# Layer 0 of a four-layer transformer: the stick-breaking heads move ahead of the causal heads, and the rotary turn moves in beside them

## The chip, the cores and the metric

The kernel runs on one core of one Trainium2 chip. The time is the device time of the whole program in microseconds (us). Five engines work from queues of their own: PE (TensorE, matrix products), DVE (VectorE), ACT (ScalarE), POOL (GpSimd) and SP (SyncE, which here only issues the loads of weights). They meet only at semaphores. TensorE runs at one of two clocks, 1.2 or 2.4 GHz; the profile gives the granted clock of a stretch as a share of 2.4 GHz, so 0.50 means 1.2 GHz.

## What is computed

Two blocks of two layers each over 512 tokens of width 1024. The change touches only the mixer of layer 0. It has 8 causal softmax heads with a rotary turn of queries and keys, and 8 stick-breaking heads without one (the causal heads' block selection is, at 512 tokens and two blocks, plain causal attention). The turn is x1\*cos - x2\*sin and x2\*cos + x1\*sin on the first 16 of a head's 64 dimensions:

```python
def attention_head_groups(h, positions, w_in, w_out):
    proj = h @ w_in
    qa, ka, va, qb, kb, vb = (t.reshape(B, T, -1, HEAD_DIM) for t in jnp.split(proj, cuts, axis=-1))
    qa = partial_rope(qa, positions)
    ka = partial_rope(ka, positions)
    oa = moba_attention(bhtd(qa), bhtd(ka), bhtd(va))
    ob = stick_breaking_attention(bhtd(qb), bhtd(kb), bhtd(vb))
    ...
    return o @ w_out

# stick-breaking, per block of 128 queries
z = einsum(q, k) * dh ** -0.5
log_1m = where(causal, log_sigmoid(-z), 0.0)
log_after = cumsum(log_1m, reverse=True) - log_1m
w = where(causal, exp(log_sigmoid(z) + log_after), 0.0)
out = einsum(w, v)
```

## The kernel before, in words

Everything lies transposed: channels on the 128 partitions, the 512 tokens along the row. The program of each engine is written out by hand, stage by stage. At the end of a stage `ph.end` drains the engine, counts up one semaphore and waits until PE, ACT, DVE and POOL have all done so: a barrier of four engines. SP has no part in it; it loads weight tiles into a ring of four slots as they come free.

Layer 0 runs these stages, each closed by such a barrier:

1. **Projection** (`pe_attn_in`, `act_attn_in`, `dve_attn_in`, lines 887 to 932). 12 weight tiles. ACT rounds tile m+1 (`next_own`, line 364), POOL takes the rest of it (line 376), PE multiplies in three passes (tiles 0 to 7 give QK1, 16 chunks of 128 channels; tiles 8 to 11 give V1, lines 420 to 422), and ACT copies the result out of PSUM (lines 918, 925). DVE weighs the adaptive-norm tiles. Before that, `dve_angles` has made the angles of the rotary turn in COS1 and SIN1 and has signalled `angles_ready`.
2. **Rotary stage** (lines 2174, 2243 to 2247, 2313 to 2314). ACT scales the stick heads' queries (QK1 chunks 8 to 11) by 0.125, takes the sine of both tables in place and puts a sign on SIN1 (`angles_done`). For each of the 8 chunks of causal queries and keys PE multiplies by a permutation (`pe_rope`, two fp32 passes of 512 columns, four PSUM buffers), and DVE does three operations of 512 columns: swapped times sin, chunk times cos, sum (`dve_rope`, lines 1194 to 1196).
3. **Causal heads** (`pe_attention`, `dve_attention`, `act_attention` over `causal_jobs`). 32 jobs, a head and 128 queries each. PE: scores (line 1034), transposes of the weights (1043), outputs (1054). DVE: scale and mask (1090, 1092), maximum (1099), reciprocal (1116), weights (1126). ACT: exponential (1152), copy of the transposes (1160), copy of the head (1167). DVE computes scores three jobs ahead before it makes the first job's weights.
4. **Stick heads** (`pe_stick`, `act_stick`, `dve_stick`, `pool_stick`, lines 1250 to 1349). Per head h, PE runs `z` (scores, line 1258, 8 instructions), `sums` (running sums by a triangle of ones, line 1268, 20 instructions) and `outputs` (line 1279, 8 instructions), in the order z(h+1), sums(h), outputs(h-1). z has two PSUM buffers; z(h) waits until ACT's `weights` of head h-2 has read its buffer (`sticks_read`). ACT runs `softplus(h+1)` (Abs, Exp, Ln over 1280 columns, lines 1299 to 1301), then `weights(h)` (Exp, line 1308), then the copy of head h-1 (line 1313). DVE has one operation a head (line 1330), POOL masks (line 1338). WORK is shared by the stages, so the barrier is needed between them.
5. **Output projection** (`pe_out`, `act_out` with a preloading of the set `natural_log_exp_and_others`, line 485, and so on).

The queues of ACT and the table sets: an activation whose function isn't in the loaded set of tables is preceded by a table load (ACT_TABLE_LOAD in the profile), placed when the program is built. `preload_act_table_set` loads a named set.

Of the kernel before, what the change touches and what calls it, by code (L numbers as in the profile page):

```python
# [9 lines left out]
ALU = mybir.AluOpType  # L10
# [81 lines left out]
def build_program(nc, w_tiles, d_tiles, xT, ctxT, positions, consts, params, rope_tables, outT):  # L92
# [12 lines left out]
    with ctx:  # L105
# [77 lines left out]
        def sig(name):  # L183

            if name not in scratch:
                scratch[name] = sem(name)
            return scratch[name]
# [721 lines left out]
                mm.then_inc(tile_done, 1)  # L909
                pe_ada_tile(pe, 0, m + ADA // 2, m % 2)  # L910

        def act_attn_in(act):
            g0 = G0["attn_in"]

            def features(m, v, i):
                next_own(act, "attn_in", round_tile, m, 2 * v, i)
                act.wait_ge(tile_done, i * 4 + (g0 + 2 * v + 1))
                act.activation(QK1[:, bass.ds(m * 2, 2), :],
                               PS[:, v * 1024:(v + 1) * 1024].rearrange("p (j c) -> p j c", j=2),
                               ACT.Copy).then_inc(evac_done, 1)  # L920
            over_pairs(act, 8, features, lambda m, v, i: None)
            for m in range(8, 12):
                next_own(act, "attn_in", round_tile, m, 2 * m, 0)
                act.wait_ge(tile_done, g0 + 2 * m + 1)
                act.activation(V1[:, :, (m - 8) * 256:(m - 7) * 256],
                               PS[:, (m % 2) * 1024:(m % 2 + 1) * 1024].rearrange("p (a c) -> p a c", a=NT),
                               ACT.Copy).then_inc(evac_done, 1)
# [322 lines left out]
        def pe_stick(pe):  # L1250
            def z(h):
                if h >= 2:
                    pe.wait_ge(sig("sticks_read"), h - 1)
                r = slice((h % 2) * 64, (h % 2) * 64 + 64)
                for i in (0, 1, 3, 2):
                    a, w = sb_bank(h, i), T - i * P

                    mm = pe.matmul(PS[:, a:a + w], QK1[r, 12 + h // 2, i * P:(i + 1) * P],
                                   QK1[r, 8 + h // 2, i * P:T], start=i != 3, stop=True, skip_group_check=True)
                mm.then_inc(sig("z_ready"), 1)  # L1260

            def sums(h):
                pe.wait_ge(sig("softplus_masked"), h + 1)
                for i in (0, 1, 3, 2):
                    for j in range(i, NT):
                        a = sb_bank(h, i) + (j - i) * P
                        w = T - j * P
                        mm = pe.matmul(PS[:, a:a + w], const("negtri") if j == i else const("negones"),
                                       SP_[h % 2][:, OFFS[j]:OFFS[j] + w], start=False, stop=True, skip_group_check=True)
                mm.then_inc(sig("sticks_ready"), 1)  # L1270

            def outputs(h):
                pe.wait_ge(sig("sticks_masked"), h + 1)
                if h >= 2:
                    pe.wait_ge(sig("stick_heads_copied"), h - 1)
                off = (h % 2) * 64
                for i in range(NT):
                    o = 3072 + (h % 2) * 512
                    mm = pe.matmul(PS[off:off + 64, o + i * P:o + T], V1[:, i, 512 + h * 64:512 + (h + 1) * 64],
                                   SW[h % 2][:, OFFS[i]:OFFS[i] + T - i * P], start=i == 0, stop=i == NT - 1,  # L1280
                                   skip_group_check=True)
                mm.then_inc(sig("stick_heads_ready"), 1)

            z(0)
            for h in range(8):
                if h + 1 < 8:
                    z(h + 1)
                sums(h)
                if h >= 1:
                    outputs(h - 1)  # L1290
            outputs(7)

        def act_stick(act, chain):
            def softplus(h):
                act.wait_ge(sig("z_ready"), h + 1)
                if h >= 2:
                    act.wait_ge(sig("sticks_ready"), h - 1)
                L, a = SP_[h % 2], (h % 2) * 1536
                chain(act.activation(L, PS[:, a:a + SBW], ACT.Abs))
                chain(act.activation(L, L, ACT.Exp, scale=-1.0))  # L1300
                act.activation(L, L, ACT.Ln, bias=SM[:, 1:2]).then_inc(sig("log_ready"), 1)

            def weights(h):
                act.wait_ge(sig("sticks_ready"), h + 1)
                if h >= 2:
                    act.wait_ge(sig("stick_heads_ready"), h - 1)
                a = (h % 2) * 1536
                act.activation(SW[h % 2], PS[:, a:a + SBW], ACT.Exp).then_inc(sig("sticks_read"), 1)

            def copy(h):  # L1310
                off = (h % 2) * 64
                act.wait_ge(sig("stick_heads_ready"), h + 1)
                act.activation(H[off:off + 64, 4 + h // 2, 0:T], PS[off:off + 64, 3072 + (h % 2) * 512:3072 + (h % 2) * 512 + T],
                               ACT.Copy).then_inc(sig("stick_heads_copied"), 1)

            softplus(0)
            for h in range(8):
                if h + 1 < 8:
                    softplus(h + 1)
                weights(h)  # L1320
                if h >= 1:
                    copy(h - 1)
            copy(7)

        def dve_stick(dve):
            for h in range(8):
                dve.wait_ge(sig("log_ready"), h + 1)
                a = (h % 2) * 1536

                dve.scalar_tensor_tensor(out=SP_[h % 2], in0=PS[:, a:a + SBW], scalar=0.0, in1=SP_[h % 2],  # L1330
                                         op0=ALU.max, op1=ALU.add).then_inc(sig("softplus_ready"), 1)

        def pool_stick(pool):
            def keep_past(buf):
# [15 lines left out]
        def rope1_chunks():  # L1350
            return [(QK1[:, x, :], const("perm_a1"), COS1, SIN1) for x in range(8)]
# [812 lines left out]
        def _(pe):  # L2164
            ph = Phase()
            pe.wait_ge(consts_loaded, 16)
            for layer in range(4):
                segs = SEG1 if layer < 2 or layer == LAST else SEG2
                if layer == 0:
# [1 line left out]
                    pe_norm_sum(pe, 0, T)  # L2171
                    pe_attn_in(pe)
                    ph.end(pe)
                    pe_rope(pe, rope1_chunks())
                    ph.end(pe)
                    pe_attention(pe, causal_jobs())
                    ph.end(pe)
                    pe_stick(pe)
                    ph.end(pe)
                    pe_out(pe, "attn_out", SEG1)  # L2180
                elif layer == 1:
# [35 lines left out]
        def _(act):  # L2217
# [5 lines left out]
            for layer in range(4):  # L2223
# [14 lines left out]
                    for k in range(DC):  # L2238
                        act_norm_chunk(act, [CTX] if layer == LAST else [MAIN, CTX], mod[:, 0:DC, :], k, "chunk_shifted")
                if layer == 0:  # L2240
                    act_attn_in(act)
                    ph.end(act)
                    act.wait_ge(sig("angles_ready"), 1)
                    act.activation(QK1[:, 8:12, :], QK1[:, 8:12, :], ACT.Copy, scale=0.125)
                    chain(act.activation(COS1, COS1, ACT.Sin))
                    chain(act.activation(SIN1, SIN1, ACT.Sin))
                    act.activation(SIN1, SIN1, ACT.Copy, scale=const("sign")).then_inc(sig("angles_done"), 1)
                    ph.end(act)
                    act_attention(act, causal_jobs(), chain)
                    ph.end(act)  # L2250
                    act_stick(act, chain)
                    ph.end(act)
                elif layer == 1:
                    act_gdn_in(act)
# [36 lines left out]
        def _(dve):  # L2291
# [6 lines left out]
            for layer in range(4):  # L2298
# [10 lines left out]
                if layer == 0:  # L2309
# [1 line left out]
                    dve_attn_in(dve, chain)  # L2311
                    ph.end(dve)
                    dve.wait_ge(sig("angles_done"), 1)
                    dve_rope(dve, rope1_chunks(), chain)
                    ph.end(dve)
                    dve_attention(dve, causal_jobs(), chain)
                    ph.end(dve)
                    dve_stick(dve)
                    ph.end(dve)
                    dve_out(dve, "attn_out", mod[:, 2 * DC:3 * DC, :], SEG1)  # L2320
                elif layer == 1:
# [38 lines left out]
        def _(pool):  # L2360
            ph = Phase()
            for layer in range(4):
                segs = SEG1 if layer < 2 or layer == LAST else SEG2
                if layer == 0:
                    for k in range(DC - 1):
                        pool_add(pool, k, T)
                    rest_tile(pool, "attn_in", 0, 0, 0)
                    pool_rest(pool, "attn_in")
                    ph.end(pool)
                    ph.end(pool)  # L2370
                    ph.end(pool)
                    pool_stick(pool)
                    ph.end(pool)
                elif layer == 1:
                    rest_halves(pool, 0, 0)
                    pool_gdn_in(pool)
                    ph.end(pool)
                    pool_gdn_prep(pool)
                    ph.end(pool)
                    for grp in range(2):  # L2380
                        pool_gdn_inverse(pool, grp)
                        ph.end(pool)
                        ph.end(pool)
                    ph.end(pool)
                else:
                    for _ in range(6):
                        ph.end(pool)
# [186 lines left out]
```

## Time and profile before

| | |
|---|---|
| median of 3 timed runs | 4042.73 us (4042.47 to 4046.4) |
| profiled execution: its time | 4048.2 us |
| profiled execution: span of the core | 4046.3 us |
| mean granted clock over the span | 0.927 |
| PE busy | 3630.5 us (90%) |
| DVE, ACT, POOL busy | 1887.5, 1249.2, 1060.4 us (47%, 31%, 26%) |
| layer 0's mixer: projection ends, rotary, causal, stick, output projection begins | 238.4, 258.0, 369.5, 462.8 us |

Busy times and durations are those of one profiled execution. A PE that is busy isn't a PE at its peak: at 1.2 GHz the same matmul keeps it busy nearly twice as long. In the rows below, "x8" counts instructions that the timeline has merged; the bracket at a row's end is how long the engine had been idle before it and what ended that.

### The profile page before, as it was taken

The numbers are of one execution on the slowest core, as the hardware profiler recorded it, in microseconds if no ns is written. First come the engines' busy times: TensorE is split into PE (matmuls) and PEld (weight loads), VectorE is DVE, ScalarE is ACT, GpSimd is POOL, SyncE is SP. The second block draws the span as 40 slices with busy tenths as digits, with TensorE's granted clock in tenths as the row PEclk, the third lists the DMA queues.
The fourth block names the chain that finished last, engine by engine and source line by source line (L and its number), as shares of the span: only waits on it lengthen the run. The fifth ranks groups of instructions, "written<-read, shape, count | busy, mean of one in ns | idle before, by whom it ended". The sixth has DMA issues, their size and how long they took to land. (4 is left out here: it accounts for less than half of the span.)

```text
span 4046.3 us, 46564 instructions
## 1 busy us (share of the span) xinstructions
PE 3630.5 (90%) x17568; PEld 2825.1 (70%) x17568; DVE 1887.5 (47%) x3523; ACT 1249.2 (31%) x1790; POOL 1060.4 (26%) x611
## 2 busy tenths in 40 slices
PE   2989999999967879999998978899999998879998
PEld 2865678878656758886575546788899566557887
DVE  7343242437354457473607683654345517662111
ACT  2224532223321132123004544222244104443222
POOL 2300334444424333433000002334400000014444
PEclk9975999999988989999997978999999997779999
DMA  6410134432200014342110001334445210002221
GB/s 229 166 73 1 42 139 147 187 120 89 88 1 1 1 52 175 142 169 96 52 66 8 1 1 42 114 144 173 148 164 172 73 73 1 1 32 83 89 98 64
DMA packets 54942, 355.62 MB, mean 88 GB/s; under 512 B 5888, under 2 KB 6912, under 8 KB 19456
## 3 DMA queue, kind: packets, MB, share of 16 engines
q1 hardware_dynamic: 54496, 351.35, 23.7%
q8 instruction: 107, 1.75, 0.2%
q10 hardware_dynamic: 288, 2.10, 0.1%
q14 instruction: 51, 0.42, 0.0%
HBM read 351.32 MB, written 2.10 MB: 87 GB/s over the span
## 5 line engine op out<-in xcount | busy, mean ns | idle before, releaser
L376 POOL TENSOR_TENSOR W_LO<-ring,W_HI 128x2048 fp32r<-128x2048 f32 (+1 forms) x177 | 730.3, 4126 | 1095.2 <-ACT W_HI L364 1095.2
L432 PE MATMUL PS<-H_HI,W_HI 128*128 128x512 f32 (+1 forms) x1888 | 713.4, 378 | 32.6 <-DVE H_LO L810 26.3
L434 PE MATMUL PS<-H_HI,W_LO 128*128 128x512 f32 (+1 forms) x1888 | 703.4, 373 | 0.0
L433 PE MATMUL PS<-H_LO,W_HI 128*128 128x512 f32 (+1 forms) x1888 | 703.3, 373 | 0.0
L364 ACT ACTIVATE W_HI<-ring 128x2048 fp32r<-128x2048 f32 (+1 forms) x214 | 366.2, 1711 | 444.6 <-PE PS L422 444.3
L432 PEld LDWEIGHTS PS<-H_HI,W_HI 128*128 128x128 f32 x1888 | 359.7, 191 | 98.6 <-issue 37.6
L434 PEld LDWEIGHTS PS<-H_HI,W_LO 128*128 128x128 f32 x1888 | 359.3, 190 | 63.4
L433 PEld LDWEIGHTS PS<-H_LO,W_HI 128*128 128x128 f32 x1888 | 360.0, 191 | 59.5 <-issue 0.2
L852 DVE SCALAR_TENSOR_TENSOR PS<-ring,SC,PS 128x256 f32<-128x256 f32 x792 | 388.0, 490 | 27.8
L420 PE MATMUL PS<-HID_HI,W_HI 128*128 128x512 f32 (+1 forms) x880 | 325.3, 370 | 4.9 <-DVE W_LO L376 4.0
L422 PE MATMUL PS<-HID_HI,W_LO 128*128 128x512 f32 (+1 forms) x880 | 323.7, 368 | 0.0
L421 PE MATMUL PS<-HID_LO,W_HI 128*128 128x512 f32 (+1 forms) x880 | 323.7, 368 | 0.0
L521 POOL TENSOR_TENSOR W_LO<-ring,W_HI 128x512 fp32r<-128x512 f32 x16 | 23.2, 1452 | 1121.6 <-ACT W_HI L511 1121.3
L592 ACT ACTIVATE GATED<-PS 128x512 f32<-128x512 f32 (+1 forms) x110 | 61.1, 555 | 724.4 <-PE PS L434 724.4
L283 PE MATMUL PS<-H,ring 128*128 128x512 f32 (+1 forms) x800 | 278.2, 511 | 6.0 <-ACT H L960 6.0
L607 DVE TENSOR_TENSOR HIDDEN<-GATED,PS 128x512 f32<-128x512 f32 (+1 forms) x110 | 69.8, 634 | 424.2 <-ACT GATED L592 424.2
L1034 PE MATMUL PS<-BIG 64*128 64x256 f32 (+5 forms) x640 | 245.8, 625 | 10.6 <-DVEq L243 7.6
L283 PEld LDWEIGHTS PS<-H,ring 128*128 128x128 f32 x800 | 152.8, 191 | 131.8 <-issue 122.2
L729 DVE SCALAR_TENSOR_TENSOR X<-PS,MOD,X 128x512 f32<-128x512 f32 (+1 forms) x80 | 55.7, 696 | 387.8 <-PE PS L422 387.8
L1054 PEld LDWEIGHTS PS<-WORK,BIG 128*64 128x64 f32 x1312 | 172.8, 162 | 90.7 <-issue 53.3
L1054 PE MATMUL PS<-WORK,BIG 128*64 128x128 f32 x1312 | 218.3, 322 | 18.6 <-ACT WORK L1160 18.3
L1160 ACT ACTIVATE WORK<-PS 128x768 f32<-128x768 f32 (+5 forms) x152 | 96.0, 631 | 314.6 <-PE PS L1043 314.5
(280 smaller groups left out, 5674.1 us busy)
## 6 DMA issues: line engine op xcount, KB each, us to landing
ring<-w_tiles SPq DMA_DIRECT2D x273, 1024.0 KB, 4.8
ring<-d_tiles SPq DMA_DIRECT2D x80, 704.0 KB, 4.1
X<-xT SPq DMA_DIRECT2D x1, 2048.0 KB, 19.3
WORK<-rope_tables ACTq DMA_DIRECT2D x2, 1024.0 KB, 6.9
outT<-H SPq DMA_DIRECT2D x8, 256.0 KB, 2.2
CN<-consts SPq DMA_DIRECT2D x1, 1377.0 KB, 15.8
X<-ctxT SPq DMA_DIRECT2D x1, 1024.0 KB, 21.5
PR<-params SPq DMA_DIRECT2D x1, 465.5 KB, 3.4
```

Of the source, the lines that this page charges most:

```text
L283: mm = pe.matmul(PS[:, o:o + w], ring[:, slot, k * 256 + j * P:k * 256 + (j + 1) * P], src[:, k, c0:c0 + w], start=k == 0, stop=k == DC - 1)
L364: act.activation(W_HI[:, b, 0:w], ring[:, g % SLOTS, 0:w], ACT.Copy).then_inc(sig("tile_rounded"), 1)
L376: eng.tensor_tensor(W_LO[:, b, 0:w], ring[:, g % SLOTS, 0:w], W_HI[:, b, 0:w].bitcast(F32), ALU.subtract).then_inc(sig("tile_split"), 1)
L420: pe.matmul(PS[:, o:o + w], hi(k), x_hi(k), start=k == 0, stop=False)
L421: pe.matmul(PS[:, o:o + w], hi(k), x_lo(k), start=False, stop=False)
L422: mm = pe.matmul(PS[:, o:o + w], lo(k), x_hi(k), start=False, stop=k == n - 1)
L432: pe.matmul(to, hi[:, cols(k, j)], x_hi(k), start=k == 0, stop=False)
L433: pe.matmul(to, hi[:, cols(k, j)], x_lo(k), start=False, stop=False)
L434: mm = pe.matmul(to, lo[:, cols(k, j)], x_hi(k), start=False, stop=k == n - 1)
L852: ins = dve.scalar_tensor_tensor(out=out, in0=w, scalar=c[:, k:k + 1], in1=acc, op0=ALU.mult, op1=ALU.add)
L1034: mm = pe.matmul(PS[:, a:a + k.shape[-1]], job["q"][m], k, start=True, stop=True)
L1054: mm = pe.matmul(PS[off:off + 64, o:o + P], v, PT[n % 2][:, x * P:(x + 1) * P], start=x == 0, stop=x == len(job["v"]) - 1)
```

## The change

The stick heads become the second stage, and the rotary stage is gone as a stage of its own:

- The scaling of the stick queries moves into ACT's projection loop, after the rounding at m == 9. The two sines and the sign move there too, after the rounding at m == 10, in a new function `act_sines`, which ends with a preload of the set `natural_log_exp_and_others`.
- `pe_stick` gets `swap(n)`: the permutation product of causal chunk n = h, issued between z(h+1) and sums(h), into PSUM columns 3584 to 4095. From n = 1 it waits for `swap_read`, DVE's reading of the chunk before.
- To make room for it, the stick heads' outputs use one PSUM bank at 3072 rather than two; even and odd heads still lie on different halves of the partitions.
- `dve_stick` gets `rotate(n)`, the three operations of the turn for chunk n = h, right after the head's one operation.
- The order of stages on all engines is projection, stick, causal, output projection: three barriers instead of four.

```diff
+        def act_sines(act, chain):
+            act.wait_ge(sig("angles_ready"), 1)
+            chain(act.activation(COS1, COS1, ACT.Sin))
+            chain(act.activation(SIN1, SIN1, ACT.Sin))
+            act.activation(SIN1, SIN1, ACT.Copy, scale=const("sign")).then_inc(sig("angles_done"), 1)
+            act.preload_act_table_set("natural_log_exp_and_others")
...
             for m in range(8, 12):
                 next_own(act, "attn_in", round_tile, m, 2 * m, 0)
+                if m == 9:
+
+                    act.wait_ge(evac_done, E0["attn_in"] + 8)
+                    act.activation(QK1[:, 8:12, :], QK1[:, 8:12, :], ACT.Copy, scale=0.125)
+                if m == 10:
+                    act_sines(act, chain)
...
-                    o = 3072 + (h % 2) * 512
+                    o = 3072
...
+            def swap(n):
+
+                if n:
+                    pe.wait_ge(sig("swap_read"), n)
+                chunk, perm, _, _ = rope1_chunks()[n]
+                pe.matmul(PS[:, 3584:3584 + T], perm, chunk, start=True, stop=True).then_inc(sig("head_swapped"), 1)
+
             z(0)
             for h in range(8):
                 if h + 1 < 8:
                     z(h + 1)
+                swap(h)
                 sums(h)
...
-        def dve_stick(dve):
+        def dve_stick(dve, chain):
+            def rotate(n):
+                c, _, cos, sin = rope1_chunks()[n]
+                tmp = ROPE_TMP[:, (n % 2) * T:(n % 2) * T + T]
+                dve.wait_ge(sig("head_swapped"), n + 1)
+                dve.tensor_tensor(tmp, PS[:, 3584:3584 + T], sin, ALU.mult).then_inc(sig("swap_read"), 1)
+                chain(dve.tensor_tensor(c, c, cos, ALU.mult))
+                dve.tensor_tensor(c, c, tmp, ALU.add)
+
...
+                rotate(h)
...
-                    pe_rope(pe, rope1_chunks())
+                    pe_stick(pe)
                     ph.end(pe)
                     pe_attention(pe, causal_jobs())
-                    ph.end(pe)
-                    pe_stick(pe)
                     ph.end(pe)
```

The programs of ACT, DVE and POOL are put in the same order.

## Rows read from the trace of the kernel before

**Rows 1.** The page, part 1: busy time of TensorE over the span.
```profile
PE 3630.5 (90%) x17568; PEld 2825.1 (70%) x17568; DVE 1887.5 (47%) x3523; ACT 1249.2 (31%) x1790; POOL 1060.4 (26%) x611
```

**Rows 2.** Windows by stage: length, busy PE, PEld, DVE, ACT, POOL, clock, DMA, GB/s.
```profile
200.00:238.00 38.00, 37.62 (x316) 37.53 (x314) 8.12 (x18) 7.36 (x6) 9.24 (x2) 1.00 0.43 166
238.00:258.00 20.00, 10.76 (x16) 3.24 (x16) 15.47 (x26) 4.12 (x5) 0.00 (x0) 0.78 0.14 52
258.00:369.00 111.00, 106.07 (x304) 59.22 (x304) 49.79 (x152) 40.81 (x128) 0.00 (x0) 0.50 0.00 1
369.00:462.00 93.00, 81.95 (x289) 47.76 (x288) 11.93 (x8) 65.56 (x56) 16.60 (x64) 0.87 0.00 0
```

**Rows 3.** Timeline of the rotary stage: start, length, engine, line, operation.
```profile
238.43 3.70 PE L1186 MATMUL PS<-BIG,CN 128*128 128x512 f32 x8 [0.81 <-ACTq L243]
238.51 1.91 ACT L2244 ACTIVATE BIG<-BIG 128x2048 f32<-128x2048 f32 x1 [0.17 <-POOLq L243]
...
241.64 0.72 ACT L2247 ACTIVATE BIG<-BIG,CN 128x512 f32<-128x512 f32 x1
242.45 0.69 DVE L1194 TENSOR_TENSOR WORK<-PS,BIG 128x512 f32<-128x512 f32 x1 [4.17 <-ACTq L243]
243.06 0.68 DVE L1195 TENSOR_TENSOR BIG<-BIG 128x512 f32<-128x512 f32 x1
243.77 0.69 DVE L1196 TENSOR_TENSOR BIG<-BIG,WORK 128x512 f32<-128x512 f32 x1
...
257.26 0.69 DVE L1196 TENSOR_TENSOR BIG<-BIG,WORK 128x512 f32<-128x512 f32 x1
258.05 4.64 PE L1034 MATMUL PS<-BIG 64*128 64x128 f32 x10 [5.67 <-DVEq L243]
```

**Rows 4.** Timeline of ACT in the projection, m == 10: the rounding and the copy.
```profile
214.32 1.91 ACT L364 ACTIVATE W_HI<-ring 128x2048 fp32r<-128x2048 f32 x1
225.36 1.03 ACT L925 ACTIVATE BIG<-PS 128x1024 f32<-128x1024 f32 x1 [9.13 <-PE PS L422]
```

**Rows 5.** Groups by line, stick stage: ACT's table loads, busy and mean ns.
```profile
L1301 ACT ACT_TABLE_LOAD x8 | 10.3, 1283 | 0.1
...
L1308 ACT ACT_TABLE_LOAD x7 | 9.0, 1283 | 0.1
```

**Rows 6.** Timeline of the stick stage: one head's round on PE and ACT.
```profile
424.16 4.60 PE L1268 MATMUL PS<-WORK,CN 128*128 128x512 f32 x20
424.27 1.24 ACT L1299 ACTIVATE WORK<-PS 128x1280 f32<-128x1280 f32 x1 [1.76 <-PE PS L1258]
...
428.69 2.37 PE L1279 MATMUL PS<-WORK,BIG 128*64 128x512 f32 x8
...
430.80 1.24 ACT L1308 ACTIVATE WORK<-PS 128x1280 f32<-128x1280 f32 x1
...
432.08 2.42 PE L1258 MATMUL PS<-BIG 64*128 64x512 f32 x8 [1.02 <-ACT WORK L1308]
...
434.55 1.24 ACT L1299 ACTIVATE WORK<-PS 128x1280 f32<-128x1280 f32 x1 [1.90 <-PE PS L1258]
```

**Rows 7.** Timeline of the stick stage: its first head on ACT and PE.
```profile
374.23 1.24 ACT L1299 ACTIVATE WORK<-PS 128x1280 f32<-128x1280 f32 x1 [4.82 <-PE PS L1258]
...
382.28 3.93 PE L1268 MATMUL PS<-WORK,CN 128*128 128x512 f32 x7 [5.00 <-POOL WORK L1338]
```

**Rows 8.** Windows: where the clock falls and where it comes back.
```profile
246.00:250.00 4.00, 3.56 (x4) 1.01 (x4) 3.93 (x7) 0.00 (x0) 0.00 (x0) 0.50 0.00 0
...
384.00:389.00 5.00, 4.50 (x19) 3.13 (x17) 1.49 (x1) 3.55 (x4) 1.04 (x4) 0.84 0.00 0
```

**Rows 9.** Timeline of the causal stage: its first transpose on PE.
```profile
264.77 0.47 PE L1043 MATMUL PS<-CN,WORK 128*128 128x128 f32 x1 [2.09 <-DVE WORK L1126]
```

**Rows 10.** Windows of layer 2's attention, early and late in its stage.
```profile
2160.00:2180.00 20.00, 16.95 (x75) 11.95 (x74) 13.07 (x39) 5.81 (x15) 0.00 (x0) 0.50 0.00 0
...
2240.00:2260.00 20.00, 18.93 (x109) 12.57 (x108) 14.07 (x30) 10.49 (x26) 0.00 (x0) 1.00 0.01 2
```

More of the change, by code:

```diff
@@ L910, in pe_attn_in, with act_attn_in @@
                 pe_ada_tile(pe, 0, m + ADA // 2, m % 2)
-        def act_attn_in(act):
+        def act_sines(act, chain):
[4 more added lines that the diff above has]
+            act.preload_act_table_set("natural_log_exp_and_others")
+        def act_attn_in(act, chain):
             g0 = G0["attn_in"]
@@ L1312, in copy @@
                 act.wait_ge(sig("stick_heads_ready"), h + 1)
-                act.activation(H[off:off + 64, 4 + h // 2, 0:T], PS[off:off + 64, 3072 + (h % 2) * 512:3072 + (h % 2) * 512 + T],
+                act.activation(H[off:off + 64, 4 + h // 2, 0:T], PS[off:off + 64, 3072:3072 + T],
                                ACT.Copy).then_inc(sig("stick_heads_copied"), 1)
@@ L2240, in _ @@
                 if layer == 0:
-                    act_attn_in(act)
+                    act_attn_in(act, chain)
                     ph.end(act)
[L2243 to L2247, printed above, removed]
+                    act_stick(act, chain)
                     ph.end(act)
                     act_attention(act, causal_jobs(), chain)
-                    ph.end(act)
-                    act_stick(act, chain)
                     ph.end(act)
@@ L2313, in _ @@
                     dve.wait_ge(sig("angles_done"), 1)
-                    dve_rope(dve, rope1_chunks(), chain)
+                    dve_stick(dve, chain)
                     ph.end(dve)
                     dve_attention(dve, causal_jobs(), chain)
-                    ph.end(dve)
-                    dve_stick(dve)
                     ph.end(dve)
@@ L2369, in _ @@
                     ph.end(pool)
+                    pool_stick(pool)
                     ph.end(pool)
-                    ph.end(pool)
-                    pool_stick(pool)
                     ph.end(pool)
```

## The prediction, made before the changed kernel was run

> **What bounds the kernel now.** I read the views in this order: the page, the windows by stage, then the timelines of the stages that move. Over the whole span TensorE is busy nine tenths [rows 1], but the change moves only stages in which it isn't the one limit. The windows by stage are read one against the other [rows 2]: the projection's end keeps TensorE full at 2.4 GHz; the rotary stage lasts 20 us with TensorE busy 10.8; the causal stage lasts 111 us with TensorE busy 106 but at 1.2 GHz throughout; the stick stage lasts 93 us with TensorE busy 82 and ACT 66.
>
> The rotary stage is bound by DVE: TensorE starts at 238.43, DVE starts its first product at 242.45 and its last sum at 257.26, and the causal scores start at 258.05 [rows 3]. The first 4 us are ACT's scaling and sines, 238.51 to 242.36; the rest is 8 chunks of three DVE operations.
>
> In the stick stage a head's round is read on PE and ACT side by side [rows 6]. From sums to sums PE runs sums 4.5 (424.16 to 428.69), outputs 2.4, then idles 1.02 for ACT's weights, then z 2.4. On ACT the round from Abs to Abs is 434.55 - 424.27 = 10.28 us; from Abs to the weights it is 430.80 - 424.27 = 6.53, and two table loads of 1.283 are in it [rows 5]. So ACT's chain with its loads sets the pace by 1.02 us over PE's own work of 9.26.
>
> **The rotary stage as a stage: -19.6.** It goes with its barrier: 258.05 - 238.43 = 19.62 us [rows 3]. What it did must now hide elsewhere.
>
> **Scaling and sines in the projection: 0.** The four operations took 242.36 - 238.51 = 3.85 us [rows 3]: 1.91 of scaling, 1.94 of sines and sign. The new load adds 1.28 [rows 5]. At m == 10 ACT rounds at 214.32 and then idles 9.13 before the copy at 225.36 [rows 4]; the sines and the load need 3.2 of that, at m == 9 the scaling 1.9 of the like gap. They stand behind the rounding on ACT's queue, so POOL and the next tile don't wait for them; behind them stands only the copy. If that cover were gone it would cost 5.1 us. `angles_ready` came before the projection, so that wait is free.
>
> **Swap on PE: +1.0 a head, into a gap of 1.02.** The 8 merged rotary instructions took 3.70 us, about 0.43 apart at full clock [rows 3]; a swap is two of them and a change of weights, 0.9 to 1.1; I take 1.0. The next z behind it waits for the weights anyway.
>
> **Table loads in the stick stage: off ACT, and PE takes over as the limit.** The 15 loads of these two lines, and one more for the first Exp of head 1, are 16 x 1.283 = 20.5 us of ACT [rows 5]. After the preload Exp and Ln are in one set. From Abs to weights ACT then needs 6.53 - 2.57 = 3.96 us. PE needs, from the end of z, swap 1.0 and sums 4.5 = 5.5, so weights start when the sums end. While ACT takes 1.24 for them, PE runs outputs for 2.4, and the 1.02 us of idle [rows 6] is gone. The new round is PE's own: 2.4 + 1.0 + 4.5 + 2.4 = 10.25 us against 10.28. Of 20.5 us taken off ACT, nothing comes out in the steady rounds; it pays for the swap. Even if the loads stayed, the swap would fit the old gap.
>
> **DVE in the stick stage: 0.** A rotate is three operations a little over 0.6 apart, 1.9 to 2.0 us [rows 3]. It waits for `head_swapped`, 1.0 after the end of z, and so ends 3.0 after it; the next softplus comes off ACT at 3.96. Queued behind the wait is only that operation. DVE is busy 12 of the 93 us there [rows 2] and would become 28.
>
> **Start of the stick stage: -3.7, of which I take -3.0.** ACT's first Abs came at 374.23 after 4.82 us of waiting, since z ran at 1.2 GHz; z takes 2.4 at full clock [rows 6, 7], and the stage now follows the projection at 2.4 GHz: -2.4. One table load of the first softplus is on the way to the first sums (8.05 us after the first Abs, 382.28 - 374.23 [rows 7]): -1.28. Against it: PE then has z of head 1 and a swap, 3.4 us, to fill 6.8, and idles 3.4. In the rotary stage TensorE was done at 242.13, could go on only after DVE's first sum at 244.46, and was at 1.2 GHz from 246 on [rows 3, 8], and in the stick stage of before it came back at the first sums [rows 8]. A fall in the first two heads costs up to 4.7 us (sums at half clock), before had some of this too. Bounds: -4.7 and +1.
>
> **Causal stage: -0.5.** It did not show a start at full clock, so I bound this. It begins with scores and then waits until DVE has scores for three jobs: the first transpose came at 264.77, 6.7 us after the stage began, mostly DVE's work [rows 3, 9]. Scores at full clock may take 1.5 us off, or nothing. After these sparse microseconds I expect 1.2 GHz as before, for the remaining 104 us. The stage's table load for Exp falls away too, beside DVE's lead. The output projection starts from 1.2 rather than 2.4 GHz, but waits for its weight pieces first: 0, plus or minus 1.5.
>
> **Sum.** -19.6 + 0 + 0 - 3.0 - 0.5 = -23.1 us. The profiled execution's 4048.2 becomes 4025.1. It lies 5.5 above the median of the three runs, so for the median: 4042.7 - 23.1 = 4019.6. A measurement of this kernel can tell about 0.2%, 8.1 us, from no change. The forecast's own range adds the bounds (-27.8 to -17.1) and 2 us for the spread of the runs, 3.9 us from first to last: 4013 to 4028.
>
> What a table load costs is where the skill and the trace part. The trace leaves it 1.283 us: in 6.53 us there are two loads and three activations of at least 1.24 each, 6.3 in all, with 0.2 left [rows 5, 6]. The Trainium skill (ScalarE: Activation LUTs, What ACT_TABLE_LOAD costs) adds a drain of about 1.38 us to each switch of sets, 2.66 in all. By it the first softplus would gain 2.66 rather than 1.28 and the sum would be -24.5; the rows leave no room for it.
>
> **Rivals.**
>
> *The causal stage gets the full clock.* Price: a head takes TensorE 106.07 / 8 = 13.3 us at 1.2 GHz [rows 2]. At 2.4 GHz that halves to 6.6, DVE has 49.79 / 8 = 6.2, and the hand-overs between them stay; I estimate 8. Each warm head saves 5.3 us, 7 of them 37: 3982; if the clock rises half way, about 18: 4001. For it: in layer 2 the same attention program stood at 1.2 GHz early in its stage and at 2.4 GHz later, with PE busy 17 of 20 us before and 19 after [rows 10], and PE is as busy in the causal stage. Now that stage is entered at full clock rather than from the idle of the rotary stage. Against: it stayed at 0.50 for all of its 111 us [rows 2], the clock fell in the rotary stage after a shorter sparse stretch than the one before the first transpose [rows 3, 8, 9], and its jobs are smaller than layer 2's. By the Trainium skill (TensorE: Matmul & The Clock Gate, Part 4: PE-mode transpose) transposes don't count as busy in the way that other matmuls do, which would make this case rarer. Layer 2 holds the full clock with transposes in every job [rows 10], so I leave the chance as it is. 20%.
>
> *The turn isn't hidden.* If DVE's three operations came between one head's softplus and the next (a wait for the swap that comes late, with the head's masking behind it), each head would pay about 2 us: 16 in all, 4035.6. Against: the order above leaves 1 us of slack, DVE is nearly idle. 5%.
>
> *Slower: the stick stage loses the clock for good.* Its rounds are now PE's own work. If the idle of the first head brings TensorE to 1.2 GHz and it stays there, a round is nearly twice 10.25; z went from 2.4 to 4.8 us between the clocks [rows 6, 7]. That is about 9 us a head, 72 in all: 4092. It takes more than two and a half heads at half clock (23.1 / 9) before the change loses. Against: before entered this stage at 1.2 GHz and got 2.4 within the first sums [rows 8]. 3%.
>
> That the change doesn't do what it says, the loads staying, gives about 1.3 us less and is in the forecast's range.
>
> **How the numbers follow.** Forecast 72% (4013 to 4028), warm causal stage 20% (3980 to 4012), turn not hidden 5%, slower 3%. The range 3988 to 4028 holds most of the first and over half of the second. Faster by over 0.2% is the first two, 92%; within 0.2% the third, 5%; slower 3%.
>
> **What would show it.** Right: no line between the projection's end and z; first Abs about 2.5 us into the stick stage; rounds of 10.2 to 10.3 us with no table load and no idle of PE before z; stick stage 89 to 92 us; causal stage 110 us at 0.50. Wrong: clock above 0.5 in the causal stage, which alone can move the time by more than 10 us; PE waiting for DVE's reading of the swap; DVE's rotate ending after the next Ln; or the projection's tiles more than 12 us apart.

## The result, and the profile after

| | before | after |
|---|---|---|
| time, median (lowest to highest) | 4044.57 us (4042.47 to 4048.43, 4 runs) | 3994.16 us (3986.77 to 4020.85, 4 runs) |
| profiled execution, its time | 4048.2 us | 3992.96 us |
| causal stage, its length | 110.6 us | 77.5 us |
| stick stage, its length | 92.4 us | 89.8 us |
| rotary stage | 19.6 us | gone |

The ratio is 0.9886, with a 95% interval of 0.984 to 0.9933. In the profiled executions the stages account for the difference: 19.6 of the rotary stage, 2.6 of the stick stage, 33.1 of the causal stage, together 55.3 us; the times differ by 4048.2 - 3992.96 = 55.2. (What lies outside these stages differs by 1 to 2 us in either direction and cancels here.) So the largest part came from a stage whose work, but for one table load, was not touched. Two executions of later variants that took 6913.64 and 13174.75 us, far above the rest of their kernel's, are left out of the medians below. A stage is measured from its first matmul to the start of its last one.

The page of the changed kernel, part 1, which answers to [rows 1]. ACT has 16 instructions and 20.8 us less, the table loads that went:

```profile
PE 3586.6 (90%) x17568; PEld 2805.6 (70%) x17568; DVE 1888.4 (47%) x3523; ACT 1228.4 (31%) x1774; POOL 1060.9 (27%) x611
```

Windows by stage of the changed kernel, with the columns of [rows 2]: the projection's end, the stick stage, then the causal stage in four parts:

```profile
200.00:236.00 36.00, 36.00 (x302) 35.94 (x301) 7.82 (x16) 11.75 (x11) 9.26 (x2) 1.00 0.45 176
236.00:327.00 91.00, 83.51 (x305) 48.25 (x304) 28.28 (x35) 45.65 (x41) 17.60 (x64) 0.94 0.03 12
327.00:332.00 5.00, 3.36 (x10) 1.40 (x10) 3.53 (x11) 2.36 (x7) 0.00 (x0) 1.00 0.00 0
332.00:360.00 28.00, 26.97 (x77) 14.92 (x77) 14.28 (x45) 9.61 (x31) 0.00 (x0) 0.51 0.00 1
360.00:380.00 20.00, 19.46 (x95) 10.75 (x96) 15.48 (x49) 13.34 (x44) 0.00 (x0) 1.00 0.01 2
380.00:406.00 26.00, 22.07 (x124) 13.56 (x124) 15.73 (x49) 15.22 (x49) 0.00 (x0) 1.00 0.00 1
```

The third column from the end is the clock. Before, it was 0.50 for all 111 us of the causal stage. Here it falls 5 us after the stage begins, as the forecast had it, but it is back at full from 360 on, which the forecast did not have. In the half-clock window 77 matmuls take 26.97 us, in the next 95 take 19.46.

ACT in the projection, m == 10 and the tile after, which answers to [rows 4]:

```profile
214.52 0.62 ACT L914 ACTIVATE BIG<-BIG 128x512 f32<-128x512 f32 x1
...
216.58 1.28 ACT L917 ACT_TABLE_LOAD   x1
223.76 1.02 ACT L938 ACTIVATE BIG<-PS 128x1024 f32<-128x1024 f32 x1 [5.89 <-PE PS L422]
```

The sines and the load stand in the wait ahead of the copy, and 5.89 us of that wait are left. The copies of three tiles start at 211.80, 223.76 and 235.72: 11.96 apart, and so were they before (213.40, 225.36, 237.32).

The start of the stick stage, all engines, which answers to [rows 3] and [rows 7]:

```profile
236.83 4.04 PE L1271 MATMUL PS<-BIG 64*128 64x512 f32 x16 [0.81 <-ACTq L243]
239.35 1.24 ACT L1320 ACTIVATE WORK<-PS 128x1280 f32<-128x1280 f32 x1 [2.61 <-PE PS L1271]
...
245.04 1.96 POOL L1368 TENSOR_SCALAR_AFFINE_SELECT WORK<-WORK 128x128 f32<-128x128 f32 x4 [25.72 <-DVE WORK L1359]
245.41 0.72 DVE L1352 TENSOR_TENSOR BIG<-BIG 128x512 f32<-128x512 f32 x1
...
247.06 3.35 PE L1281 MATMUL PS<-WORK,CN 128*128 128x512 f32 x4 [5.14 <-POOL WORK L1368]
```

z follows the projection's barrier, the first Abs comes 2.5 us in, and the first sums wait for POOL's four masks, which run while DVE turns the first chunk of causal queries.

One round in its middle, which answers to [rows 6]:

```profile
279.82 4.50 PE L1281 MATMUL PS<-WORK,CN 128*128 128x512 f32 x20
...
284.24 2.37 PE L1292 MATMUL PS<-WORK,BIG 128*64 128x512 f32 x8
284.35 1.24 ACT L1329 ACTIVATE WORK<-PS 128x1280 f32<-128x1280 f32 x1 [1.46 <-PE PS L1281]
286.54 2.42 PE L1271 MATMUL PS<-BIG 64*128 64x512 f32 x8
288.89 1.12 PE L1302 MATMUL PS<-BIG,CN 128*128 128x512 f32 x2
289.00 1.24 ACT L1320 ACTIVATE WORK<-PS 128x1280 f32<-128x1280 f32 x1 [1.76 <-PE PS L1271]
```

No bracket stands behind a line of PE, so PE waits for nobody, and ACT now waits for PE twice a round (1.46 and 1.76). DVE's part, in the same round:

```profile
281.34 0.69 DVE L1353 TENSOR_TENSOR BIG<-BIG,WORK 128x512 f32<-128x512 f32 x1
282.93 1.49 DVE L1359 SCALAR_TENSOR_TENSOR WORK<-PS,WORK 128x1280 f32<-128x1280 f32 x1 [0.89 <-ACT WORK L1322]
```

The last step of the turn ends at 282.03 and DVE then waits 0.89 for the next softplus, about the 1 us of slack that was forecast. The round, Abs to Abs, is 289.00 - 278.96 = 10.04 us.

### The profile page after: what moved, and what is told of

Read it like the earlier page. It is cut to its first block and busy times, and to the rows that moved or that the text cites. A ratio compares the mean times of both kernels' runs of the same rounds, so it can differ in the third digit from the quotient of the medians.

```text
span 3990.8 us, 46542 instructions
## 1 busy us (share of the span) xinstructions
PE 3586.6 (90%) x17568; PEld 2805.6 (70%) x17568; DVE 1888.4 (47%) x3523; ACT 1228.4 (31%) x1774; POOL 1060.9 (27%) x611
## 5 line engine op out<-in xcount | busy, mean ns | idle before, releaser
L852 DVE SCALAR_TENSOR_TENSOR PS<-ring,SC,PS 128x256 f32<-128x256 f32 x792 | 388.0, 490 | 27.8
L1047 PE MATMUL PS<-BIG 64*128 64x256 f32 (+5 forms) x640 | 229.9, 593 | 5.6 <-DVE WORK L1103 2.2
L1067 PE MATMUL PS<-WORK,BIG 128*64 128x128 f32 x1312 | 202.6, 306 | 19.8 <-ACT WORK L1173 19.6
L1067 PEld LDWEIGHTS PS<-WORK,BIG 128*64 128x64 f32 x1312 | 161.3, 153 | 82.4 <-ACT WORK L1173 45.8
L420 PEld LDWEIGHTS PS<-HID_HI,W_HI 128*128 128x128 f32 x880 | 165.9, 188 | 34.6 <-DVE W_LO L376 5.3
```

Of the source, the lines that this page charges most:

```text
L420: pe.matmul(PS[:, o:o + w], hi(k), x_hi(k), start=k == 0, stop=False)
L852: ins = dve.scalar_tensor_tensor(out=out, in0=w, scalar=c[:, k:k + 1], in1=acc, op0=ALU.mult, op1=ALU.add)
L1047: mm = pe.matmul(PS[:, a:a + k.shape[-1]], job["q"][m], k, start=True, stop=True)
L1067: mm = pe.matmul(PS[off:off + 64, o:o + P], v, PT[n % 2][:, x * P:(x + 1) * P], start=x == 0, stop=x == len(job["v"]) - 1)
```

## Experiments

**The same kernel again, and the spread of the runs.** The expectation:

> The changed kernel once more, unaltered, for the spread of its times. Theory A (the causal stage of layer 0 gets the full clock at a point that differs from run to run; in the first profile it rose after two of its eight heads): times lie in two groups or a band, near 4021 us where the stage stays at 1.2 GHz and from 3985 to 4005 us where it rises, and the mean granted clock of a run goes with its time (0.926 in the slow ones, 0.936 to 0.940 in the others). Rival B (the stage rises because it is entered from the stick stage, always at the same place): all runs within 4 us of each other, near 3990 us.

Measured: a median of 4019.02 us over 6 runs, 3991.63 to 4024.77; ratio 0.991 (0.9884 to 0.9936). The profiled one was 4024.1 us. Its windows, the first microseconds of the causal stage and the rest:

```profile
326.00:330.00 4.00, 3.40 (x10) 1.40 (x10) 2.80 (x9) 1.55 (x6) 0.00 (x0) 0.95 0.02 4
330.00:436.00 106.00, 101.39 (x294) 56.62 (x294) 46.72 (x144) 38.43 (x123) 0.00 (x0) 0.50 0.00 0
```

This is the forecast's case: the stage lasted 109.3 us, the stick stage 88.2. A third set of the same kernel:

> The changed kernel unaltered, for more of its times. So far 5 of 10 runs near 3987 to 3998 and 5 near 4018 to 4025; of the kernel before, 9 of 40 runs below 4041. If the share of runs with the rise is the same for both kernels (a quarter): 1 to 4 of some ten runs below 4010. If entering the stage at full clock helps: half of them or more.

Measured: 3993.83 us, 6 runs of 3990.97 to 3997.77, none of the other sort; ratio 0.9882 (0.9844 to 0.9921). In its profile the clock is low at the same place and comes back at 372, after the third head:

```profile
331.00:372.00 41.00, 40.13 (x114) 22.18 (x114) 20.32 (x64) 14.40 (x47) 0.00 (x0) 0.50 0.00 0
372.00:410.00 38.00, 34.26 (x181) 20.12 (x180) 25.12 (x78) 23.53 (x75) 0.00 (x0) 1.00 0.00 1
```

All 16 runs of the changed kernel fall in two groups: 11 between 3986.8 and 3997.8 (median 3993.6), 5 between 4018.0 and 4024.8 (median 4020.85), nothing between. The three profiles put the groups down to the causal stage: 77.5 us (3992.96), 83.1 us (3994.06) and 109.3 us (4024.1). The share differs from set to set: 3 of 4, 2 of 6, 6 of 6. The second and the third were taken on different chips, so that a part of the difference may be the chip's or the hour's.

The kernel before was run beside every experiment: of 71 runs, 54 lie above 4041 (median 4046.8), 7 between 3999.0 and 4011.1, 10 between 4027.5 and 4040.0. No trace of one of the 17 faster ones was kept. That the clock rose in them, in the 10 later than in the 7, is inferred: their mean granted clocks are 0.934 to 0.942 in the 7 and 0.928 to 0.931 in the 10, and 0.922 to 0.929 in all but one of the 50 slower ones for which it is on record. Beside the third set of the changed kernel, where 6 of 6 rose, 2 of 14 of the kernel before lay below 4041; beside the second, where 2 of 6 rose, it was 4 of 19.

**The order alone.** Causal and stick stage change places on PE, ACT, DVE and POOL (here PE); the rotary stage, the loads and the sines stay:

```diff
+                    pe_stick(pe)
+                    ph.end(pe)
                     pe_attention(pe, causal_jobs())
-                    ph.end(pe)
-                    pe_stick(pe)
```

> The kernel before with the causal and the stick stage exchanged and nothing else: the rotary stage stands where it did, the table loads stay. The causal stage is now entered at 2.4 GHz from the stick stage. Theory A (where the clock rises is a matter of where the stage falls in time, not of what stood ahead of it): most runs within 5 us of before, some up to 35 us faster. Rival B (entering from the stick stage is what warms it): 20 to 35 us faster in nearly every run. Rival C (the order itself gives the start of the stick stage at full clock): 2 to 3 us at the most, causal stage at 0.50.

Measured: 4047.1 us, 11 runs; ratio 0.9995 (0.9983 to 1.0008). Two of the 11 were at 4020.9 and 4022.7. The profiled execution was one of those, and the clock came back after 41 us:

```profile
355.00:396.00 41.00, 40.22 (x114) 22.17 (x114) 20.24 (x64) 14.38 (x47) 0.00 (x0) 0.50 0.00 1
396.00:434.00 38.00, 34.24 (x181) 20.12 (x180) 25.11 (x78) 23.53 (x75) 0.00 (x0) 1.00 0.00 1
```

So entering the causal stage from the stick stage does not suffice: 9 of 11 times show no rise, and in the profiled one, which entered at full clock, the clock fell within the stage's first 5 us all the same. Its set is the one in which the changed kernel rose in 2 of 6 runs only; beside the set of 6 of 6 this order alone was not run.

**TensorE kept busy at the start of the causal stage.** Products of 512 columns into a bank of PSUM that nobody reads, between the first scores and the first transpose, 1 + 5 in the kernel before, 1 + 3 in the changed one:

```diff
+        def pe_keep_busy(pe, n):
+            for _ in range(n):
+                pe.matmul(PS[:, 2560:3072], ones, CN[:, 0:512], start=True, stop=True, skip_group_check=True)
...
+                    if s == 1:
+                        pe_keep_busy(pe, busy[0])
+                if n == 0:
+                    pe_keep_busy(pe, busy[1])
                 if n >= 1:
                     outputs(n - 1)
                 turn(n)
```

> The kernel before, with 6 products (constants by constants, fp32, 512 columns) into an unused PSUM bank while DVE computes the first scores of layer 0's causal stage: one after the second score product, five before the first transpose. They are extra work, some 10 us of it at 1.2 GHz, of which up to 3 us lie in TensorE's idle time. If the causal stage stays at the full clock once it has it: it rises within the first 10 us of the stage and the whole is 28 to 38 us faster than before. If the stage's own density always brings it back to 1.2 GHz: 4 to 8 us slower than before.

> The changed kernel, with 4 such products at the start of the causal stage (one after the second score product, three before the first transpose), in TensorE's idle time at 2.4 GHz. If the sparse first microseconds are what costs the causal stage its clock: granted clock 1.00 through the stage, all runs within a few us of each other, 3978 to 3986 us, faster than the changed kernel in its best run. If not: the same spread as the changed kernel, plus 0 to 1 us.

Measured: before with them 4004.59 us (4004.28 to 4007.93, 4 runs), ratio 0.9895 (0.9881 to 0.9909); after with them 3981.7 us (3979.04 to 3982.92, 5 runs), ratio 0.9838 (0.9826 to 0.9851). This is the fastest kernel of the study that computes everything and is fast in every run. The windows of the causal stage in the kernel before with them, then in the changed one:

```profile
257.00:269.00 12.00, 11.97 (x19) 5.30 (x20) 5.65 (x17) 2.98 (x7) 0.00 (x0) 0.51 0.00 1
269.00:331.00 62.00, 57.58 (x295) 33.26 (x294) 43.39 (x135) 37.83 (x121) 0.00 (x0) 1.00 0.00 1
```

```profile
326.00:330.00 4.00, 3.48 (x10) 1.48 (x10) 2.08 (x7) 1.52 (x5) 0.00 (x0) 1.00 0.02 4
330.00:394.00 64.00, 59.58 (x303) 34.44 (x302) 46.77 (x146) 38.53 (x123) 0.00 (x0) 1.00 0.00 1
```

Before, the clock is back 12 us into the stage; after, it never falls. The same heads, with the same products, take 67.4 us at full clock against 109.3 at half: a head is 8.4 us. The first transpose of the changed kernel came at 333.27, 6.8 us after the stage's start, so the extra products held the start up by about 1.4 us against the 5.4 without them and gave back 42.

**One extra product, or one in each job.** In the changed kernel a single one before the first transpose, (0, 1) in place of (1, 3); in the kernel before a short one of 128 columns in each of the 32 jobs:

```diff
+                if dense:
+                    pe.matmul(PS[:, 2560:2688], ones, CN[:, 0:128], start=True, stop=True, skip_group_check=True)
```

> The changed kernel with a single such product ahead of the first transpose of the causal stage instead of four. If the four are needed: the clock falls at the stage's start and the times spread as those of the changed kernel, 3985 to 4025. If a little is enough: 3979 to 3983 in every run.

> The kernel before with one more product (constants, fp32, 128 columns, into an unused PSUM bank) in each of the 32 jobs of layer 0's causal stage, ahead of the outputs, where TensorE passes from one kind of product to the next: 0.43 us each at 1.2 GHz, so up to 14 us of work added to TensorE, which is the limit of the stage at 1.2 GHz. If the stage at 1.2 GHz is only just too sparse to be given the full clock: it rises in nearly every run and the kernel is 10 to 30 us faster than before, in spite of doing more. If the clock depends on how the stage is entered: no rise, 5 to 14 us slower.

Measured: with the single one 3980.93 us, 6 runs, but two of the six at 4020.91 and 4023.23, the profiled one among the late ones (causal stage 109.3 us at 0.50). With one in each job 4029.3 us (4023.45 to 4036.74), all 12 runs; ratio 0.9977 (0.9955 to 0.9999). The windows of the latter:

```profile
257.00:293.00 36.00, 34.18 (x91) 19.24 (x92) 17.42 (x52) 11.01 (x34) 0.00 (x0) 0.50 0.00 1
293.00:347.00 54.00, 52.10 (x278) 32.55 (x277) 32.71 (x101) 29.79 (x94) 0.00 (x0) 1.00 0.00 1
```

A kernel that does the whole work of before and 32 products more is faster than before mostly is (4046.8; the median beside it was 4044.2). In the profiled run the clock came up after 36 us of the stage; no trace of the other 11 was kept, but all of them lie between 4023 and 4037, where a run without the rise would lie above 4041, so a rise in each is likely, in some at a later point.

**A later causal stage.** A copy of 1280 columns on ACT at the end of the stick stage, to move the stage's start:

```diff
                     act_stick(act, chain)
+                    act.activation(WORK[:, 0:SBW], WORK[:, 0:SBW], ACT.Copy)
                     ph.end(act)
```

> The changed kernel with one copy of 1280 columns on ACT at the very end of the stick stage: the causal stage begins some 1.3 us later and is otherwise the same. So far 11 of 16 runs of the changed kernel have the clock rise in the causal stage (3987 to 3998 us) and 5 don't (4018 to 4025). If the rise hangs on where the stage lies against the points in time at which the clock can change, and these points lie alike in most runs: the share changes, or the rises come at another head, so that the groups move by a good 5 us. If the share is a property of the stage alone: two thirds of the runs at 3988 to 4000, the rest at 4019 to 4027.

Measured: the stage began 2.3 us after the stick stage's end in place of 1.0. Of 11 runs 4 were between 3986.17 and 3997.96, 7 between 4020.54 and 4030.21; median 4020.9, ratio 0.9942 (0.9905 to 0.9978). 4 of 11 against 11 of 16 is too little to say that the shift did it, the more so as these runs come from yet another chip. Inconclusive.

**The table loads.** With the extra products in place, so that the causal stage is the same in every run, the preload of the common table set is left out, and with it the loads come back in every head:

```diff
-            act.preload_act_table_set("natural_log_exp_and_others")
```

> The changed kernel with the busy start of the causal stage (so that its clock doesn't blur the comparison), and without the preload at the end of the sines: the table loads stay in the stick stage. My step (PE's own work of 10.2 us a head is the limit, the loads' worth of ACT is free but for one): 1 to 2 us slower than the same kernel with the preload (3981.7), rounds of 10.0 to 10.3 us. Rival (ACT's chain still counts): over 5 us slower.

Measured: 3983.61 us (3982.54 to 3985.32, 4 runs), 1.9 above the median of the kernel with the preload. The middle of a round on ACT and PE:

```profile
292.53 1.28 ACT L1329 ACT_TABLE_LOAD   x1
293.82 1.36 ACT L1329 ACTIVATE WORK<-WORK,SM 128x1280 f32<-128x1280 f32 x1
...
296.50 1.24 ACT L1336 ACTIVATE WORK<-PS 128x1280 f32<-128x1280 f32 x1
297.79 2.42 PE L1278 MATMUL PS<-BIG 64*128 64x512 f32 x8 [0.16 <-ACT WORK L1336]
```

z waits for ACT's weights by only 0.16: with swap and loads both there ACT's chain sets the round, at 10.28 us, and PE's own work, 10.04, is close behind. The stick stage is 2.5 us longer than with the preload (92.0 against 89.5); the two medians come from different sets.

The other half: the kernel before with the extra products and the preload, but no swap in its stick stage.

```diff
                     ph.end(act)
+                    act.preload_act_table_set("natural_log_exp_and_others")
                     act_stick(act, chain)
```

> The kernel before with the busy start of its causal stage, and a preload of the set with Exp and Ln ahead of its stick stage: the table loads' part of the change alone. My step (PE's own work, 9.26 us a head, takes the place of ACT's 10.28): rounds of 9.2 to 9.3 us, the stick stage 7 to 9 us shorter than in the same kernel without it (89.7), 3996 to 3998. Rival (all of the loads come out): 20 us.

Measured: 4000.74 us (3997.87 to 4003.8, 6 runs), ratio 0.9896 (0.9862 to 0.9931). z to z, with no wait on PE:

```profile
376.41 2.42 PE L1266 MATMUL PS<-BIG 64*128 64x512 f32 x8
385.59 2.42 PE L1266 MATMUL PS<-BIG 64*128 64x512 f32 x8
```

The round is 9.18 us and the stage 82.1 against 89.7, 7.6 less. The medians, from different sets, differ by 3.9 only, the spans of the profiled executions by 10; what of the 7.6 was given back elsewhere in most runs isn't settled.

**The turn left out.** Swap and rotate are gone from the stick stage, so the rotary turn of the causal heads is not computed at all:

```diff
-                swap(h)
                 sums(h)
...
-                rotate(h)
```

> The same kernel with the busy start, with the swap on TensorE and the turn on DVE left out of the stick stage (the rotary turn isn't computed). This is the price of the hidden work. My step: TensorE's round falls by the swap alone, 0.8 to 1.0 us a head, 6 to 8 us in all, 3974 to 3976; what DVE does costs nothing. Rival (the turn isn't hidden on DVE): 16 us or more.

Measured: 3971.32 us (3970.24 to 3973.26, 4 runs), 10.4 below the kernel with the turn. The stick stage lasted 81.7 us against 89.5, with a round of 9.18: 7.8 us. The other 2.6 lie outside the stage and aren't explained. POOL's masks in the first head:

```profile
246.37 1.04 POOL L1374 TENSOR_SCALAR_AFFINE_SELECT WORK<-WORK 128x128 f32<-128x128 f32 x4 [25.73 <-DVE WORK L1366]
```

**The stick stage's start kept busy as well.** Five more of these products ahead of its first sums:

```diff
                 swap(h)
+                if h == 0:
+                    for _ in range(5):
+                        pe.matmul(PS[:, 3072:3072 + T], ones, CN[:, 0:512], start=True, stop=True, skip_group_check=True)
                 sums(h)
```

> The changed kernel with the busy start of the causal stage, and five such products also ahead of the first sums of the stick stage, in the 5 us in which TensorE waits for the first softplus. If the clock of the stick stage's first heads is lost by that idle: no fall below 1.00 in the stage, first two rounds at 10 us, 2 to 5 us faster than 3981.7. If the falls come from the wait for the first weights as well: 0 to 2 us faster. A start of the first sums delayed by the products would make it 0 to 1 us slower.

Measured: 3983.16 us (3976.14 to 3987.56, 6 runs), no gain on 3981.7. Its windows of the first and the second head:

```profile
248.00:255.00 7.00, 5.67 (x25) 3.80 (x24) 0.94 (x1) 1.24 (x1) 2.08 (x8) 1.00 0.01 2
255.00:262.00 7.00, 7.00 (x14) 3.56 (x13) 3.42 (x4) 3.87 (x3) 0.07 (x1) 0.52 0.00 0
```

In the kernel without the five, the stage has two short falls, and the first begins while the first sums are still waited for:

```profile
245.70:249.10 3.40, 2.81 (x4) 1.47 (x5) 1.88 (x2) 0.63 (x1) 1.59 (x5) 0.50 0.00 0
256.00:259.40 3.40, 3.40 (x5) 1.47 (x5) 1.29 (x2) 3.26 (x3) 0.00 (x0) 0.50 0.00 0
```

With them the first fall is gone, but the second lasts 6.8 us (255.0 to 261.8) instead of 3.4: as much time at half clock as before in sum. The stage is as long as it was, 89.7 us.

## Why the prediction was right or wrong

**The range held, the likeliest case did not.** The forecast was 4019.6, the median is 3994.16, and it lies in the range only because the range was drawn over a part of the first rival. There is luck in that too: the next six runs of the same kernel had a median of 4019.02, almost the forecast's number. The step that failed is the causal stage, put at -0.5 because 1.2 GHz was expected "for the remaining 104 us", and with it the chance of the first rival, 20%. The stage measured -33.1: in the profiled run the low clock lasted 27 us. "It stayed at 0.50 for all of its 111 us" was read as a property of the stage. It was one throw: by its times the same kernel before rises in a part of its runs (17 of 71 below 4041), and with 32 short products more all 12 runs lay below 4037. The mechanism was in the text, with [rows 10] as its evidence: the same program at 0.50 and later at 1.00 in one stage. Its price was about right, too: assumed 8 us a head, measured 8.4, and a clock that rises after two or three of eight heads gave 3987 to 3998, between the rival's 3982 (all but one head) and 4001 (half way). What the prediction lacked was an answer to how firm the 0.50 was: three runs within 4 us of each other didn't show that the same kernel can also end at 3999.0.

**Like with like the sum was good.** Where the clock didn't rise in either kernel, 4020.85 - 4046.8 = -25.9 us against the -23.1 of the sum. By its terms:

- Rotary stage, -19.6: right. z starts after the same 0.81 us of idle as the rotary products did.
- Scaling and sines in the projection, 0: right. Tiles 11.96 apart.
- Swap and loads, rounds of 10.2 to 10.3: right in kind, 10.04 measured. The terms of PE's round, start to start, are 4.42, 2.30, 2.35 and 0.97 against the 4.5, 2.4, 2.4 and 1.0 of the sum. (These add up to 10.3; the 10.25 of the text is 9.26 + 1.0.) The 2.4 were durations with their modelled ends, and the sums themselves are 4.53 without a swap ahead of them and 4.42 with one, so that a swap costs a steady round 0.86, not 1.0: 10.04 against 9.18. Loads that stay cost 1.9 us in the medians, 2.5 in the stage (1.3 predicted). That the loads pay for the swap is shown from both sides: without the swap the round is 9.18 us, with neither swap nor preload it was 10.28, and with both 10.04.
- Stick stage's start, -3.0: the stage lost 2.6, 4.2 and 3.0 us in three profiles. The first Abs came 2.2 us earlier in the stage (4.73 us after its start before, 2.52 after), near the 2.4 worked out. The first sums came 247.06 - 239.35 = 7.71 us after the first Abs, not 8.05 - 1.28 = 6.77: most of the load's 1.28 was given back by POOL's masks, 1.96 us instead of 1.04. In the kernel without the turn the distance was 6.79. The prediction's sum had no term for this. The short fall of the clock in the first heads was there (0.50 at 243.8 to 250.6 and 257.4 to 260.8).
- Causal stage at 1.2 GHz, -0.5: 110.6 to 109.3, so -1.3, within its bounds, in the run where the clock did not rise. In the first profiled run the first transpose came 5.4 us in rather than 6.7:

```profile
327.64 3.38 PE L1047 MATMUL PS<-BIG 64*128 64x128 f32 x10 [0.71 <-ACTq L243]
...
333.03 0.47 PE L1056 MATMUL PS<-CN,WORK 128*128 128x128 f32 x1 [2.01 <-DVE WORK L1139]
```

Two readings were off without moving the forecast. TensorE was not at 1.2 GHz throughout "from 246 on" in the rotary stage: it was back at full from 252.5 to 255.9. And the bounds as listed add up to -27.3 at the lower end, not -27.8.

**The other rivals.** The turn is hidden from DVE's side: no round of PE waits for DVE. But it isn't free: left out, the stick stage is 7.8 us shorter, because PE is the limit and pays 0.86 a steady round for the swap; the rest is in the first rounds. The third rival, a stick stage that loses the clock for good, did not happen: the clock came back within 7 us. And the transposes in every one of its jobs did not keep the causal stage from holding the full clock to its end.

**The drain at a switch of table sets**, the 1.38 us that the Trainium skill (ScalarE: Activation LUTs, What ACT_TABLE_LOAD costs) adds to each load, does not show here. The runs side with the trace: in the kernel whose loads stay the Ln starts at 293.82, 1.29 after its load began, with no room for 1.38 more.

**What stays open** is why the changed kernel rises in 11 of 16 runs and the kernel before in 17 of 71. Shown is that enough extra work at the stage's start decides it: all 29 runs of the six kernels that have it lie in a narrow band (4004 to 4008 and 3998 to 4004 in the two made from the kernel before, 3970 to 3988 in the four made from the changed one), and the six traces have the full clock in the causal stage from its start or from 11 to 12 us on. Shown is too that the order of the stages alone does not do it (2 of 11), and that the full clock, once there, stays: in all ten traces that have it in the causal stage it lasts to the stage's end, with fewer busy microseconds of PE (59.58 of 64) than the stage has at half clock. The half clock lasts to the end in four traces and gives way in six. That the stage's place in time matters is only argued; the delayed stage didn't settle it, and the part of the chip was not separated. Nor was it separated whether the extra products act by their work or by the 1.4 us by which they hold up the first transpose; against the second speaks that a stage begun 1.3 us later rose in 4 of 11 runs only.

## What to carry to other kernels

Don't take the clock of one profile as a property of a stage: look at the spread of the runs, and where TensorE has work throughout a stage that runs at half clock, fill the sparse microseconds at its start with products into an unused bank; four of them were worth 14 us in the median here (3995.3 over all 16 runs of the changed kernel, 3981.7 with them) and made the time steady. When work is taken off the limiting engine of a round, work out which one is next: 20.5 us off ACT shortened the stick stage by 2.5 while the swap stood on PE, and by 7.6 without it. Work moved beside other work also meets it on the idle engines: price the short steps on the path again, not only the busy shares.

## What the runs showed of the hardware

- At full clock the causal stage had TensorE busy 59.58 of 64 us and kept the clock to its end. At half clock it was busy 101.39 of 106 and, in that run, stayed at half to its end; with the same work the clock rose after 32 and 45 us of the stage in two others.
- POOL's four masks of 128x128 took 1.96 us while DVE ran the rotary operations on SBUF, and 1.04 without them, on the path to the first sums. The Trainium skill (GPSIMD Engine Reference, Specifications) says that VectorE and GpSimd share SBUF interfaces and get in each other's way when a DVE instruction has two inputs in SBUF; the rows agree with it, and two of a turn's three operations are of that kind (BIG<-BIG and BIG<-BIG,WORK). One mask alone takes 0.29 us. Of the four, the first two began beside the turn's first operation, which has an input in PSUM, and took 0.29 each; the other two met the second and third operation. One mask's shortest, middle and longest time over the stage, in ns, before and after:

```profile
L1338 POOL TENSOR_SCALAR_AFFINE_SELECT WORK<-WORK x64: 292/294/297, 381.2 to 459.4; 128x128 f32<-128x128 f32 x64
L1368 POOL TENSOR_SCALAR_AFFINE_SELECT WORK<-WORK x64: 292/292/763, 245.0 to 324.2; 128x128 f32<-128x128 f32 x64
```

- In the kernel with the extra products a run that does more is the faster one: 32 products added to the kernel before took its median from 4044.2 to 4029.3 us.
